# Two-block transformer on one core: the second block's mixers, with the out-projection in three parts and the queues in another order

## The reference

```python
sh1, sc1, g1, sh2, sc2, g2 = split(c_act @ ada_w[l] + ada_b[l])
h = rmsnorm(x, norm_mix_g[l]) * (1.0 + sc1) + sh1
u = h @ w_in[l]                       # 1024 x 2564: fox q k v f, pool, retention q k v g, conv
y_fox  = softmax(causal(q @ k.T * scale + cq[:, None] - ck[None, :])) @ v   # ck, cq: cumulated log_sigmoid(f + fb)
y_pool = mix(windowed_mean(pu) - pu) * pool_scale
y_ret  = silu(rg) * groupnorm(decay_masked(rope(rq) @ rope(rk).T) @ rv) * gn_g
y_conv = silu(layernorm(conv31(a * sigmoid(gate)) + conv_b))
x = x + g1 * (concat([y_fox, y_pool, y_ret, y_conv]) @ w_out[l])
x = x + g2 * ffn(rmsnorm(x, norm_ffn_g[l]) * (1.0 + sc2) + sh2)
```

## Time and profile before

| what | us |
|---|---|
| median of 3 runs | 2362.66 (2360.11 to 2364.32) |
| the profiled execution, its own time | 2358.11 |
| its span, first to last instruction | 2356.8 |
| TensorE busy | 2222.1 (94%) |
| TensorE weight load busy, beside it | 1463.6 (62%) |
| VectorE busy | 713.1 (30%) |
| ScalarE busy | 418.5 (18%) |
| mean granted TensorE clock | 0.963 of full |

### The profile page before, as it was taken

One profiled execution on the slowest core, in us unless ns is written; L12 is line 12 of the kernel. 1 busy time (PEld: TensorE's weight loads), 2 busy tenths in 40 slices (PEclk: granted clock), 3 DMA queues, 4 the chain that ended last, 5 costly groups with the idle time before them and its releaser, 6 DMA issues.

```text
span 2356.8 us, 36800 instructions
## 1 busy us (share of the span) xinstructions
PE 2222.1 (94%) x16161; PEld 1463.6 (62%) x16161; DVE 713.1 (30%) x1471; ACT 418.5 (18%) x936; POOL 0.2 (0%) x4
## 2 busy tenths in 40 slices
PE   8988999999878999999999999889899999889998
PEld 5664777666746666455455464556577775657775
DVE  2562465215543100100100100127436623730001
ACT  2463000113551000001001010132210002220001
POOL 0000000000000000000000000000000000000000
PEclk9988999999989999999999999989799999889999
DMA  5223986032305999899899796232099532218410
GB/s 214 101 82 143 410 318 239 1 132 108 118 22 223 426 386 395 344 390 428 351 419 427 321 356 279 83 143 101 27 396 365 223 123 81 99 73 339 150 36 18
DMA packets 55174, 523.88 MB, mean 222 GB/s; under 512 B 6368, under 2 KB 6880, under 8 KB 16864
## 3 DMA queue, kind: packets, MB, share of 16 engines
q1 hardware_dynamic: 45792, 471.13, 49.3%
q10 hardware_dynamic: 9216, 50.34, 5.7%
HBM read 520.39 MB, written 1.05 MB: 221 GB/s over the span
## 4 chain that ended last, share of the span: by engine, by line
PE 86%; DVE 9%; ACT 4%; issue 1%; DMA 0%; DVEq 0%; SPq 0%; ACTq 0%
PE ps L89 86%; DVE ring L89 5%; ACT ring L89 2%; DVE stat L89 1%; DVE natural L89 1%; DVE residual L89 1%; DVE transposed L89 0%; ACT L89 0%; DMA ring<-in_moe 0%; ACT z L89 0%; ACT stat L89 0%; DVE gates L89 0%; DMA constants<-in_const 0%; ACT natural L89 0%; DVE z L89 0%
## 5 line engine op out<-in xcount | busy, mean ns | idle before, releaser
L89 PE MATMUL ps<-ring 128*32 128x256 f32 (+9 forms) x7764 | 546.3, 339 | 14.5 <-DVE ring L89 4.3
L89 PEld LDWEIGHTS ps<-ring 128*32 128x32 f32 (+4 forms) x7764 | 371.2, 124 | 184.5 <-issue 64.3
L89 PE MATMUL ps<-ring,z 128*32 128x512 f32 (+3 forms) x2048 | 474.5, 584 | 0.3 <-ACT z L89 0.3
L89 PE MATMUL ps<-ring,transposed 128*128 128x384 f32 (+4 forms) x1408 | 471.9, 492 | 0.1
L89 PE MATMUL ps<-transposed,ring 128*128 128x256 f32 x2112 | 466.4, 379 | 5.6 <-DVE transposed L89 3.3
L89 PEld LDWEIGHTS ps<-transposed,ring 128*128 128x128 f32 x2112 | 401.0, 190 | 86.1 <-issue 31.2
L89 PEld LDWEIGHTS ps<-ring,transposed 128*128 128x128 f32 x1408 | 263.6, 192 | 187.6 <-issue 65.1
L89 DVE TENSOR_TENSOR z<-z,ps 128x256 f32<-128x256 f32 (+3 forms) x146 | 58.7, 402 | 894.9 <-ACT z L89 865.6
L89 PEld LDWEIGHTS ps<-ring,z 128*32 128x32 f32 (+2 forms) x2048 | 175.5, 140 | 219.9 <-issue 209.4
L89 ACT ACTIVATE z<-ps 128x256 f32<-128x256 f32 (+2 forms) x151 | 56.4, 374 | 941.5 <-PE ps L89 941.5
L89 ACT COPY z<-ps 128x384 f32<-128x384 f32 (+6 forms) x166 | 68.0, 410 | 672.0 <-PE ps L89 670.3
(11 more groups left out here) (122 smaller groups left out, 946.7 us busy)
## 6 DMA issues: line engine op xcount, KB each, us to landing
ring<-in_moe SPq DMA_DIRECT2D x88, 2048.0 KB, 11.8
ring<-in_ffn SPq DMA_DIRECT2D x66, 1536.0 KB, 13.4
ring<-in_moe SPq DMA_DIRECT2D x88, 1024.0 KB, 10.6
ring<-in_w_in SPq DMA_DIRECT2D x26, 1536.0 KB, 6.5
z<-in_ada ACTq DMA_DIRECT2D x48, 768.0 KB, 5.8
ring<-in_w_out SPq DMA_DIRECT2D x12, 1536.0 KB, 6.9
natural<-in_ada ACTq DMA_DIRECT2D x16, 768.0 KB, 7.5
ring<-in_ple_gate SPq DMA_DIRECT2D x4, 1536.0 KB, 6.4
```

The costliest lines, as they stand in the source:

```text
L89: self.ins = None if self.book.counting else op(*args, **kw)
```

## The change

The rows of `w_out` are put in the order convolution, pooling, fox, retention, and the outputs of the mixers in `natural` likewise. The out-projection is then made in three parts (`early`: convolution and pooling, 16 of 32 matmuls; `fx` and `re`: 8 each), each with its own turn and copy and its own waits. The sums stay in PSUM banks 0, 1, 2 and 5 throughout.

The gates are spread ahead of the turn, as each bank of PSUM comes free. The bias, gains and repeated gates (`dve_adapt`, `dve_adapt_gates`) are made on VectorE ahead of the ple products in layer 0, and between feed-forward and residual in layer 1. For this the small rows are loaded when the last expert residual is done; slot 3 is free then, since the third ple gate tile goes to slot 5.

The forgetting sums along keys are made for 32 equal columns per head with a broadcast column as the stationary operand, in one PSUM bank, and copied once with a minus by ScalarE. They enter the scores by a second matmul per head that picks one row (`pick`) and adds into the same sum. VectorE adds only the query's sum and the mask, and takes the maximum; ScalarE subtracts it in the exponential (one per head) and sums beside it. The norms of convolution and retention read PSUM in place of a copy.

The steps on the three engines come in another order, some projections are cut into halves (`parts`), and the convolution's 31 taps are cut into 20, 8 and 3.

```diff
--- before.py
+++ after.py
+    two["pick"] = (np.arange(P)[:, None] % 64 == 32 * np.arange(2)[None, :])
...
-    PLE_UP_SLOT, PLE1_UP_SLOT, PLEG = 0, 8, [1, 2, 3]
+    PLE_UP_SLOT, PLE1_UP_SLOT, PLEG = 0, 8, [[1, 2, 3], [1, 2, 5]]
...
+    def dve_head_norm(x, n, width, eps, tmp, st, s, src=None):
...
-        dve(V.tensor_tensor, x, x, spread(s1_, 2, width), ALU.subtract)
+        dve(V.tensor_tensor, x, src, spread(s1_, 2, width), ALU.subtract).then_inc(f"{s}.centred")
...
-    ad_rep = Carve(work, 16000)(16, P)
+    ad_rep = Carve(zbuf, 3600)(16, P)
...
+            pe.wait_ge(*(("ple1.sig4", "ple1.sig5") if l == 0 else (f"mixb1.h{q // 2}{q % 2}",)))
...
-        dve(V.tensor_copy, fx_rep, spread(fx_lf.rearrange("p i h -> p (i h)"), 2, P)).then_inc(f"fx.rep{l}")
+        dve(V.tensor_tensor, fx_lf, fx_lf, fx_e1, ALU.subtract).then_inc(f"fx.lf{l}")
...
-        for pair in range(2):
-            pe.wait_ge(f"fx.kT{l}" if pair == 0 else f"fx.cq{l}")
-            for e in range(2):
-                hh, b = 2 * pair + e, 4 - pair
-                mm(ps[:, b, e * SEQ:e * SEQ + P], fx_rep[:, hh, :], C("tri"))
-                mm(ps[:, b, e * SEQ + P:(e + 1) * SEQ], fx_rep[:, 4 + hh, :], C("tri"), True, False)
-                mm(ps[:, b, e * SEQ + P:(e + 1) * SEQ], fx_rep[:, hh, :], C("ones"), False, True)
-            pe.then_inc(f"fx.sums{l}{pair}")
+
+        def column(i, hh):
+            return fx_lf[:, i, hh:hh + 1].to_broadcast([P, 32])
+        for tile, i, what, start, stop in ((0, 0, "tri", True, True), (1, 1, "tri", True, False), (1, 0, "ones", False, True)):
+            for hh in range(4):
+                at = 64 * (hh % 2) + 32 * (hh // 2)
+                mm(ps[at:at + 32, 4, tile * P:(tile + 1) * P], column(i, hh), C(what), start, stop)
+        pe.then_inc(f"fx.sums{l}")
...
+    def act_fx_sums(l):
+        act.part("fx")
+        act.wait_ge(f"fx.sums{l}")
+        act(S.mul, fx_ckT, ps[:, 4, 0:SEQ], -1.0).then_inc(f"fx.ckT{l}")
...
-        pe.wait_ge(f"fx.ck{l}{par}" if i == 0 else f"fx.out{l}0")
+        pe.wait_ge(f"fx.ckT{l}", f"fx.cq{l}", "const2")
+        if i:
+            pe.wait_ge(f"fx.out{l}0")
+        rows = slice(64 * par, 64 * par + 64)
         for a in range(2):
-            mm(ps[:, 4 - par, a * n:(a + 1) * n], fx_qT[64 * par:64 * par + 64, i, a, :], fx_kT[64 * par:64 * par + 64, a, 0:n])
+            mm(ps[:, 4 - par, a * n:(a + 1) * n], fx_qT[rows, i, a, :], fx_kT[rows, a, 0:n], True, False)
+            mm(ps[:, 4 - par, a * n:(a + 1) * n], C("pick")[rows, a:a + 1].to_broadcast([64, P]), fx_ckT[rows, 0:n], False, True)
...
-        dve(V.tensor_tensor, fx_cm[:, :, 0:n], spread(C("causal")[:, P * i:P * i + n], 1, 4), fx_ck[:, :, 0:n], ALU.subtract)
+        mx = stats(0)[:, 0:4]
         for par in range(2):
             dve.wait_ge(f"fx.score{l}{i}{par}")
             for a in range(2):
                 hh = 2 * a + par
                 dve(V.scalar_tensor_tensor, out=s4[:, hh, :], in0=ps[:, 4 - par, a * n:(a + 1) * n], scalar=fx_cq[:, i, hh:hh + 1],
-                    in1=fx_cm[:, hh, 0:n], op0=ALU.add, op1=ALU.add)
-        dve_softmax_shift(s4, 4, stats(0), f"fx.s{l}{i}")
+                    in1=C("causal")[:, P * i:P * i + n], op0=ALU.add, op1=ALU.add)
+        dve(V.tensor_reduce, mx, s4, AXX, ALU.max)
+        dve(V.tensor_scalar, mx, mx, -1.0, None, ALU.mult).then_inc(f"fx.s{l}{i}.max")
 
     def act_fx_softmax(l, i):
+
         act.part("fx")
-        act_softmax_exp(fx_scores(i)[1], f"fx.s{l}{i}")
+        act.wait_ge(f"fx.s{l}{i}.max")
+        for hh in range(4):
+            row = fx_scores(i)[1][:, hh, :]
+            act(S.activation, row, row, ACT.Exp, bias=stats(0)[:, hh:hh + 1], accum_out=stats(0)[:, 8 + hh:9 + hh])
+        act.then_inc(f"fx.s{l}{i}.exp")
 
     def dve_fx_sum(l, i):
         dve.part("fx")
-        dve_softmax_sum(fx_scores(i)[1], 4, stats(0), f"fx.s{l}{i}")
+        dve.wait_ge(f"fx.s{l}{i}.exp")
+        dve(V.reciprocal, stats(0)[:, 16:20], stats(0)[:, 8:12])
...
+    MIXED2 = {"early": (4, (2, 5), "cf.out{l}", "po.out{l}"), "fx": (2, (3, 3), "fx.out{l}0", "fx.out{l}1"), "re": (2, (6, 6), "re.out{l}")}
+    MIXED2_AT = {"early": 0, "fx": 4, "re": 6}
+
+    def mixed2_places(what):
+        n, banks = MIXED2[what][0:2]
+        return [(i, ps[:, banks[i], (0 if n == 4 else 2 * i * P):(4 if n == 4 else 2 * i + 2) * P], MIXED2_AT[what], n) for i in range(NT)]
+
+    def pe_turn_mixed2(l, what):
+        pe.part("turn")
+        pe.wait_ge(*(signal.format(l=l) for signal in MIXED2[what][2:]))
+        for i, place, k0, n in mixed2_places(what):
+            for k in range(n):
+                pe(T.transpose, place[:, k * P:(k + 1) * P], xn[:, i, (k0 + k) * P:(k0 + k + 1) * P], C("ident"))
+        pe.then_inc(f"outb{l}.turned.{what}")
+
+    def act_copy_mixed2(l, what):
+        act.part("turn")
+        act.wait_ge(f"outb{l}.turned.{what}", f"mixb{l}.z61")
+        for i, place, k0, n in mixed2_places(what):
+            act(S.copy, xt[:, k0:k0 + n, i * P:(i + 1) * P], place.rearrange("p (k t) -> p k t", k=n))
+        act.then_inc(f"outb{l}.xt.{what}")
+
+    BANKS1, BANKS2 = ((2, 3), (4, 5)), ((0, 1), (2, 5))
+
+    def pe_wout2(l, what, i):
+
+        pe.part("wout")
+        pe.wait_ge(f"outb{l}.xt.{what}", *(f"mixb{l}.wout{c}" for c in {"early": (0, 1), "fx": (1,), "re": (2,)}[what]))
+        k0 = MIXED2_AT[what]
+        for q in range(2):
+            for k in range(k0, k0 + MIXED2[what][0]):
+                mm(ps[:, BANKS2[i][q], :], xt[:, k, i * P:(i + 1) * P],
+                   slot(WOUT2[k // 3])[:, (k % 3) * D + q * 512:(k % 3) * D + (q + 1) * 512], k == 0, k == KD - 1)
...
+        def win(t, i, parts=(0, 1)):
+            pe_win(s, t, i, WIN2, DIN2, parts)
+        pe_adapt(l)
         pe_turn_h(s)
         win(0, 0)
         win(0, 1)
         win(1, 0)
         win(1, 1)
-        pe_adapt(l)
         win(2, 0)
         pe_cf_turn(l)
         win(2, 1)
         win(3, 0)
+        win(3, 1)
+        win(4, 0)
         pe_fx_turn(l, 0)
         pe_fx_turn(l, 1)
-        win(3, 1)
-        win(4, 0)
         win(4, 1)
-        pe_po_pool(l)
-        win(5, 0)
+        win(5, 0, (0,))
         pe_fx_sums(l)
-        pe_cf_back(l)
-        win(5, 1)
+        win(5, 0, (1,))
         pe_fx_scores(l, 0, 0)
         pe_fx_scores(l, 0, 1)
-        pe_po_mix(l)
-        win(6, 0)
+        win(5, 1, (0,))
+        pe_cf_back(l)
+        win(5, 1, (1,))
         pe_fx_weights(l, 0)
-        win(6, 1)
+        win(6, 0, (0,))
+        pe_fx_values(l, 0)
+        pe_po_pool(l)
         pe_re_turn(l, 0)
-        pe_re_turn(l, 1)
-        pe_fx_values(l, 0)
-        for hh in range(4):
-            pe_re_scores(l, hh)
         pe_fx_scores(l, 1, 0)
         pe_fx_scores(l, 1, 1)
+        pe_re_turn(l, 1)
+        pe_po_mix(l)
+        win(6, 0, (1,))
+        pe_re_scores(l, 0)
+        pe_re_scores(l, 1)
+        win(6, 1)
+        pe_re_scores(l, 2)
+        pe_re_scores(l, 3)
+        pe_turn_mixed2(l, "early")
+        pe_fx_weights(l, 1)
         pe_re_values(l)
-        pe_fx_weights(l, 1)
         pe_fx_values(l, 1)
-        pe_turn_mixed(f"outb{l}", outs2(l))
-        pe_wout(s, f"outb{l}", WOUT2)
+        pe_wout2(l, "early", 0)
+        pe_wout2(l, "early", 1)
+        pe_turn_mixed2(l, "fx")
+        pe_wout2(l, "fx", 0)
+        pe_wout2(l, "fx", 1)
+        pe_turn_mixed2(l, "re")
+        pe_wout2(l, "re", 0)
+        pe_wout2(l, "re", 1)
...
     def act_mixers2(l):
         act_modulate_xt(s, gains[:, 0:8], mod[:, 0:8])
-        for t in range(2):
-            z(t, 0)
-            z(t, 1)
         act_adapt(l)
+        z(0, 0)
+        z(0, 1)
+        z(1, 0)
+        z(1, 1)
         act_cf_gate(l)
         z(2, 0)
         act_cf_turn(l)
         z(2, 1)
         z(3, 0)
+        z(3, 1)
+        z(4, 0)
         act_fx_turn(l, 0)
         act_fx_turn(l, 1)
-        z(3, 1)
         act_fx_exp(l)
         act_fx_log(l)
-        z(4, 0)
         z(4, 1)
+        act_fx_sums(l)
+        z(5, 0)
+        act_fx_softmax(l, 0)
+        z(5, 1)
+        act_fx_weights(l, 0)
+        act_cf_root(l)
         act_po(l)
-        z(5, 0)
-        z(5, 1)
-        act_cf_root(l)
-        act_fx_softmax(l, 0)
-        z(6, 0)
-        act_fx_weights(l, 0)
-        z(6, 1)
         act_re_turn(l, 0)
         act_re_turn(l, 1)
         act_cf_out(l)
+        z(6, 0)
+        act_fx_softmax(l, 1)
+        z(6, 1)
         act_re_gate(l)
-        act_fx_softmax(l, 1)
+        act_copy_mixed2(l, "early")
         act_fx_weights(l, 1)
         act_re_root(l)
-        act_copy_xt(f"outb{l}")
+        act_copy_mixed2(l, "fx")
+        act_copy_mixed2(l, "re")
...
     def dve_mixers2(l):
-        dve_adapt(l)
         dve_norm(s)
         dve_modulate_xt(s, gains[:, 0:8], mod[:, 0:8])
-        dve_adapt_gates(l)
         dve_cf_gate(l)
-        dve_cf_conv(l, 0, 24)
+        dve_cf_conv(l, 0, 20)
         dve_fx_logit(l)
```

(85 more changed lines are left out.)

37 lines of the change are left out of this document (14 added, 23 removed).

## The result

The changed kernel takes 2321.85 us (median of 4 runs, 2319.63 to 2323.76); the kernel before, run beside it, 2361.39 (2359.42 to 2364.32). The ratio is 0.9833, 95% interval 0.9815 to 0.9850: 39.5 us faster, where 37.4 were forecast. The profiled execution took 2319.97 us, its span is 2318.7, its mean granted clock 0.976 (0.963 before).

A forecast was written before the change was run, and what follows sets the result against it. TensorE's work plus its waits and low clock bound the kernel. Per-layer section: work 117.8, waits 7.2, low clock 2.6, plus 2.5, makes 130.1; gains 16.3, 17.3 and fronts total 37.4, forecasting 2325 us, range 2314 to 2344.

The forecast's parts named there:

- Front: Stretch ahead of each mixer section's first projection, with the turn: gain of 1.1 us in layer 0, 2.7 in layer 1.
- New wait 1: TensorE ahead of the forgetting sums: waits 5.0 us for VectorE's forget values, in place of the 2.63 us wait.
- Low clock: Mixer section: 2.6 us lost behind the 5.0 us wait, between 1.3 and 9; the old stretch's 11.2 us goes.
- Rival A: From the 5 us wait to the early out-projection, clock stays low through small steps: some 10 us a layer, 2344; chance 0.14.
- B: Section's tail bound by VectorE or ScalarE: TensorE stands 3 to 5 us a layer before the early half, 2333; chance 0.10.
- C: Slower: low clock entered in the 5 us wait lasts until the early out-projection, 34 us a layer, 2388; chance 0.04.
- D: Early out-projection meets unfinished input, hides nothing; 3 to 4 us of retention wait stay, low clock at turn, 2336; chance 0.06.
- The rule on table loads: ScalarE's function-set switches at about 2.66 us each: the sum would gain about 2 us per layer less, 2329.
- the scores: Eight more matmuls of 64 rows on TensorE: +1.3 us a layer with some overlap, between +0.7 and +2.6.
- the 2.5 us: Added to the section's 127.6 us, making 130.1, because the same walk over the old order ended 2.5 short of the trace.
- VectorE's relief: Copies, broadcast, subtractions and sums removed from VectorE, some 9 us, lie beside TensorE's work: gain zero, ScalarE's exponentials likewise; up to 1.5.
- The prediction's own walk: Three engine queues stepped through behind the forget values with old durations, supply against TensorE's demand: thin margins, one 0.4 us wait.

## Why the prediction was right

It was right in sign, size and mechanism: 2325 forecast, 2321.85 measured, section 130.1 and 129.7. Its steps:

- **Front.** Layer 0 gained 1.6 from the end of the ple matmuls to W (1.1 forecast): 1.1 ahead of the turn, as forecast, and 0.5 from the turn on, which itself took 5.25 for 6.25. Layer 1 gained 2.8, forecast 2.7. Undoing the gates costs 9.7 by the medians and 11.0 by the traces; forecast were two times 3.6 and the fronts, 11.0.
- **New wait 1.** 5.15 at W+55.7, forecast 5.0 at W+55.5, released by VectorE. The wait of 0.4 at the second rotation did not come. The two waits in the out-projection are 0.87 each, forecast 0.9.
- **Low clock.** 2.4 behind the wait against 2.6, measured by itself with idle matmuls at 2.2 to 3.2. The 11.2 are gone: that it was the clock, and not only the waits, is shown by the idle matmuls in the kernel before, where the same groups took 10.0 us less (8.1 in layer 1) once the clock was up.
- **Rival A** (0.14) did not happen: the small steps ran at 1.00 for 31.5 us. In the new order no idle stood between the small steps; in layer 0 of the kernel with the sums undone there were some (0.42, 0.55, 0.83), and the clock was low behind them. The Trainium skill, "TensorE: Matmul & The Clock Gate", section "A second HAM failure mode: psum-queue depth-cycling", tells of a clock that swings because of such short idles between groups of matmuls; the two traces agree with it, but in layer 1 of that kernel the values behind a wait of 0.86 took 4.68, near full speed. **B**, **C** and **D** did not happen either: no wait ahead of the early part.
- **The rule on table loads.** A load takes 1.28 us and the next exponential starts 1.29 after the load began (1653.85, 1655.14), as in the earlier trace rows. The Trainium skill, "ScalarE: Activation LUTs", section "What ACT_TABLE_LOAD costs", counts about 2.66 us for a switch; this case's traces do not agree. In the changed kernel TensorE never waited for the exponentials.
- **Sums.** 24 records with a stationary of 32 columns take 0.86 at full clock, forecast 0.95 from the earlier trace rows.

Three terms were off. Two of them, the scores and the 2.5 us (below), offset each other nearly to nothing, which is luck. The third did not move the sum, but it is wrong as an account: **"VectorE's relief ... Zero, up to 1.5"**. The runs show some 5 to 9 us a layer in the new order (the sections grew by 4.5 and 8.5 when it was undone, though TensorE then saved the scores' 2.8 and paid only 1.9 for the wide sums). Without it there are waits of 0.4 to 1.6 at the rotations, masks, pooling and values, and low clock behind them. The prediction's own walk had margins of 0.3, 0.7, 1.2 and 0.1 us, and it seems to have held that gain already: it has the first rotation ready at W+78.0, where the trace has it ready at W+79.7 in the changed kernel and at W+82.3 with the sums undone. It never asked what the walk gives without the relief. The total was right because the walk was; the credit was not. The same holds for the order of the queues, behind which the prediction looked for the gone waits and which alone gives nothing.

**Scores**, +1.3 forecast between +0.7 and +2.6, are +2.8. Eight records of 64 rows took 0.72 without the added ones; the sixteen take 1.70 (1633.44 to 1635.14). With 256 columns it is 1.14 and 2.96. So the eight added matmuls cost their full length and a little more (0.21 and 0.43 each make 2.6), the upper bound. The overlap that the bound of +0.7 hoped for did not extend to them: with the sums undone the two halves of the rows start 0.01 us apart and run side by side, in the changed kernel the second half starts 0.55 us after the first (0.97 with 256 columns), behind five of its eight records.

**The 2.5 us that the walk missed** came to about 1: work is 129.7 - 6.9 - 2.4 = 120.4, and the forecast's 117.8 with the scores' 1.5 more is 119.3. So 1.4 less here stands against 1.5 more at the scores.

## What to carry to other kernels

Price a new order of the queues apart from the work that it comes with: here the order alone is worth nothing, and the part that relieves VectorE brings TensorE 0.9 us more of matmuls a layer (2.8 of scores for 1.9 of sums) and is still worth 9 us. When a walk over the queues ends in margins of a few tenths of a microsecond, run it again without each "free" part; what breaks shows where the gain is. A wait on the bounding engine costs its length and, behind the long ones here, low clock too, so put the chain that ends in it ahead of work that can be late (five taps instead of eleven ahead of the forget values took 14 to 16 us off), and where that can't be done, idle matmuls in the wait give the clock back.
